# Strips for the left-over rows, four gate-and-up buffers and a new order of loads in a mixture-of-experts kernel

## The reference

```python
def _swiglu(x, w_gu, w_down):
    f = w_down.shape[0]
    gu = x @ w_gu
    return (jax.nn.silu(gu[..., :f]) * gu[..., f:]) @ w_down
...
    def body(b, acc):
        rows = lax.dynamic_slice(row_tok, (b * EXPERT_BLOCK,), (EXPERT_BLOCK,))
        rw = lax.dynamic_slice(row_w, (b * EXPERT_BLOCK,), (EXPERT_BLOCK,))
        e = block_e[b]
        gu = x_pad[rows] @ w_gu[e]
        y = ((jax.nn.silu(gu[:, :f]) * gu[:, f:]) @ w_down[e]) * rw[:, None]
        return acc.at[rows].add(y)
...
    routed = _routed_experts(xt, idx, w.astype(xt.dtype), w_gu, w_down)
    shared = _swiglu(xt, sh_w_gu, sh_w_down)
    return (routed + shared).reshape(B, L, D)
```

## Time and profile before

| | us |
|---|---|
| three runs | 1251.51, 1248.92, 1253.96 |
| median | 1251.51 |
| the profiled execution | 1256.82 |
| its span in the trace | 1255.0 |
| PE busy in the span | 1189.5 (95%) |
| DVE busy in the span | 787.9 (63%) |
| first product of the experts' loop starts | 439.87 |
| down(0) starts | 458.25 |
| up of the last step starts | 1182.38 |

### The profile page before, as it was taken

How to read it: one execution, slowest core, us unless ns; L and a number is a source line. 1 busy time by engine, 2 the same in 40 slices (tenths; PEclk the granted TensorE clock), 3 DMA queues, 4 the chain that set the end, 5 groups by cost and what they waited for, 6 DMA issues and landing times.

```text
span 1255.0 us, 22626 instructions
## 1 busy us (share of the span) xinstructions
PE 1189.5 (95%) x7122; PEld 1040.6 (83%) x7122; DVE 787.9 (63%) x1625; ACT 420.8 (34%) x582; POOL 606.0 (48%) x509
## 2 busy tenths in 40 slices
PE   6999999999999799999999999999999999999973
PEld 6897989747874399999999999999999998998931
DVE  7565657388988256666665566566566655647528
ACT  5253435353441023233333233233232232323323
POOL 5222222001657455666555666666666665756310
PEclk9999999999999999999999999999999999999997
DMA  6111111403352979999999999999999999999864
GB/s 240 51 35 51 44 41 34 184 27 135 102 169 71 278 230 352 375 364 359 370 355 366 357 351 362 358 349 367 344 352 355 343 352 338 346 350 341 282 165 175
DMA packets 83587, 317.50 MB, mean 253 GB/s; under 512 B 15989, under 2 KB 32450, under 8 KB 58594
## 3 DMA queue, kind: packets, MB, share of 16 engines
q1 hardware_dynamic: 56592, 249.50, 51.4%
q0 software_dynamic: 26656, 67.23, 21.9%
q10 hardware_dynamic: 306, 0.34, 0.1%
HBM read 274.38 MB, written 51.00 MB: 259 GB/s over the span
## 4 chain that ended last, share of the span: by engine, by line
DMA 50%; PE 24%; issue 11%; DVE 9%; ACT 3%; POOL 3%; POOLq 1%; DVEq 0%; ACTq 0%; SPq 0%
DMA routed_rows<-ysb,to_row 47%; PE bank L116 6%; PE bank L117 6%; PE bank L118 6%; PE bank L957 3%; PE bank L440 2%; POOL expert_list L787 1%; DMA win_raw<-in_w_in 1%; POOL routed_rows L840 1%; DVE routed L1440 1%; DVE h L1136 1%; DVE routed L1429 1%; DMA lists<-expert_list 1%; DVE h L1134 1%; DVE h L1120 1%
## 5 line engine op out<-in xcount | busy, mean ns | idle before, releaser
L957 PEld LDWEIGHTS bank<-xT,wgu 128*128 128x128 f32 x4096 | 516.3, 192 | 21.2 <-issue 10.4
L957 PE MATMUL bank<-xT,wgu 128*128 128x160 f32 (+1 forms) x4096 | 521.0, 288 | 10.5 <-DVE xT L1317 9.6
L810 POOL DMA_INDIRECT xg<-h_rows,from_row x288 | 324.2, 1126 | 110.6 <-issue 86.7
L840 POOL DMA_INDIRECT routed_rows<-ysb,to_row x96 | 147.8, 1540 | 215.8 <-issue 210.3
L1098 ACT ACTIVATE ysb<-bank,of_row 128x512 f32<-128x512 f32 x64 | 44.0, 687 | 439.3 <-DVE to_row L1312 381.1
L1359 DVE TENSOR_TENSOR wd_lo<-wd_raw,wd_hi 128x1024 fp32r<-128x1024 f32 x128 | 151.1, 1222 | 39.9 <-ACT wd_hi L1089 39.4
L1089 ACT ACTIVATE wd_hi<-wd_raw 128x1024 fp32r<-128x1024 f32 x128 | 127.9, 1048 | 1.4 <-issue 0.6
L787 POOL DMA_INDIRECT expert_list<-entry,place x64 | 64.7, 1010 | 129.9 <-DVE place L1197 112.2
L116 PE MATMUL bank<-hT_hi,win_hi 128*128 128x348 f32 (+1 forms) x320 | 113.4, 355 | 9.7 <-DVE hT_lo L538 9.7
L352 POOL TENSOR_TENSOR win_lo<-win_raw,win_hi 128x1024 fp32r<-128x1024 f32 x16 | 43.6, 2725 | 145.6 <-ACT win_hi L463 145.5
L1302 DVE TENSOR_TENSOR picks<-lists,pick 128x20 f32<-128x20 f32 x64 | 11.9, 185 | 161.5 <-POOLq L834 111.0
(11 more groups left out here) (216 smaller groups left out, 1629.5 us busy)
## 6 DMA issues: line engine op xcount, KB each, us to landing
wgu<-in_w_gu SPq DMA_DIRECT2D x128, 1024.0 KB
wd_raw<-in_w_down SPq DMA_DIRECT2D x64, 1024.0 KB, 8.4
win_raw<-in_w_in SPq DMA_DIRECT2D x16, 512.0 KB, 3.9
xg<-h_rows,from_row POOLq DMA_INDIRECT x288
hT_raw<-in_hT SPq DMA_DIRECT2D x8, 520.0 KB, 7.4
wout_raw<-in_w_out SPq DMA_DIRECT2D x1, 4096.0 KB, 14.4
h_in<-in_h_rows SPq DMA_DIRECT2D x8, 512.0 KB, 4.0
h_rows<-h SPq DMA_DIRECT2D x8, 512.0 KB, 2.7
```

Of the source, the lines that this page charges most:

```text
L810: pool.indirect_dma_start(out=xg[b][:, g, :], out_offset=None, in_=h1_quarters, in_offset=bass.IndirectOffsetOnAxis(ap=from_row[b][:, g:g ...
L840: pool.indirect_dma_start(out=routed_rows, out_offset=bass.IndirectOffsetOnAxis(ap=to_row[b][0:r, half:half + 1], axis=0), in_=ysb[b][0:r, ...
L957: mm = pe.matmul(bank[:, 2 * f + half, 0:BLOCK[b]], wgu[b][:, f, k, c:c + P], xT[b][:, k, 0:BLOCK[b]], start=(k == 0), stop=(k == KT - 1))
```

## The change

1. **Left-over rows.** The 32 rows get a tile of their own, hid_rest (plain float32, not split), and are multiplied by wd_raw, which wd_lo of even steps no longer overwrites. There are four matmuls for c and k = 0, 1, each with a stationary operand of 32 columns, and each writes 32 partitions of its own: k and c choose the strip at partition 0, 32, 64 or 96 (`rest_at`). They stand behind all of the step's main products. ACT and DVE add the two strips of each c as before. hid_hi becomes 128 columns wide, and POOL's clearing of it is gone.
2. **Four gate and up buffers.** SP loads the gate and up weights of step t + 4 after down(t), behind the down weights of step t + 2. The loop body holds four steps, and the number of steps is rounded to a multiple of four (64 stays 64).
3. **The loop's entry.** Of the loads at `first_ready` the first four stay; the second half of wgu1 and wd_raw1 wait for `lists_loaded`, the rest of the lists for the first step's gathers (`gathered0`), and wgu2 and wgu3 follow (wgu3 after the shared products). sdn and ln_f are loaded before `first_ready`. On DVE the second shared product's gating stands behind turn(0), and PE waits for it only at the second half of up(0).
4. **The lists' shape.** COLS goes from 65 to 72 and SLOTS from 36 to 33.

The diff, cut to its core:

```diff
-SLOTS = 36
+SLOTS = 33
 MORE_MAX = -(-(SEQ - P) // P)
-COLS = E + 1
+COLS = E + 8
...
+WGU = 4
...
-    wgu = [m.at(f"wgu{j}", 16384 * j, [P, FT, KT, 2 * P], F32) for j in range(2)]
+    wgu = [m.at(f"wgu{j}", (0, 16384, 166432, 99584)[j], [P, FT, KT, 2 * P], F32)
+           for j in range(WGU)]
     wd_at, wd_hi_at = (32768, 182816), (40960, 141184)
     wd_raw = [m.at(f"wd_raw{j}", wd_at[j], [P, FT, D], F32) for j in range(2)]
-    wd_lo = [m.at(f"wd_lo{j}", wd_at[j], [P, FT, D], F32R) for j in range(2)]
+    wd_lo = [m.at(f"wd_lo{j}", (132992, wd_at[1])[j], [P, FT, D], F32R) for j in range(2)]
...
-    hid_hi = [m.at(f"hid_hi{j}", (129152, 96416)[j], [P, FT, 2 * P], F32R) for j in range(2)]
+    xT = [m.at(f"xT{j}", (85888, 91680)[j], [P, KT, SQ * GB[j]], F32) for j in range(2)]
+    hid_hi = [m.at(f"hid_hi{j}", (129152, 96416)[j], [P, FT, P], F32R) for j in range(2)]
+    hid_rest = m.at("hid_rest", 130176, [P, FT, REST[0]], F32)
...
+    def rest_at(c, k):
+
+        return (2 * c + k) * SQ
...
+    def wgu_loads(i, j):
+
+        return i * 16 // WGU + j // WGU * 16 + 16
...
-        with eng.Fori(0, n, 2) as i:
-            for b in range(2):
-                yield i, b, 4
+        with eng.Fori(0, n, WGU) as i:
+            for j in range(WGU):
+                yield i, j, 4
...
+        sp.wait_ge(h1_stored, 16 * TILES)
+        sp.wait_ge(routed_begun, 16 * TILES)
+        sp.wait_ge(turned, TILES)
+        sp.dma_start(sdn[:, :, :], sh_down.rearrange("(k p) c -> p k c", p=P)
+                     ).then_inc(sdn_loaded, 16)
+        for j in range(2):
+            sp.dma_start(ln_f[j][:, :], ln[2 + j:3 + j, :].to_broadcast([P, D])
+                         ).then_inc(lnf_loaded, 16)
...
         load_wgu(0, 1, 0)
+        sp.wait_ge(lists_loaded, 16 * NQ)
         load_wgu(0, 1, 1)
-        sp.wait_ge(h1_stored, 16 * TILES)
-        sp.wait_ge(routed_begun, 16 * TILES)
         load_wd(0, 1)
-        sp.wait_ge(lists_loaded, 16 * NQ)
+        sp.wait_ge(gathered[0], 16 * GB[0])
         for q in range(NQ):
             sp.dma_start(lists[q * SQ:(q + 1) * SQ, FIRST:, :],
                          expert_list.rearrange("(a c) w -> a c w", a=SQ)[:, FIRST:, :]
                          ).then_inc(lists_rest_loaded, 16)
-        for f in range(FT):
-            sp.wait_ge(up_done, UPS + 2 * f + 2)
-            load_wgu(0, 2, f)
+        load_wgu(0, 2, 0)
+        load_wgu(0, 2, 1)
+        sp.wait_ge(sh_up, 2 * FT)
+        load_wgu(0, 3, 0)
+        load_wgu(0, 3, 1)
         sp.wait_ge(sched_loaded, 16)
         for i, j, more in steps(sp):
-            for f in range(FT if more >= 3 else 0):
-                sp.wait_ge(up_done, (i + j) * UPS + 2 * UPS + 2 * f + 2)
-                sp.sem_inc(sp_pass, 1)
-                load_wgu(i, j + 3, f)
             if more >= 2:
                 sp.wait_ge(down_done, DOWNS[1] + before(DOWNS, i, j + 1))
                 sp.sem_inc(sp_pass, 1)
                 load_wd(i, j + 2)
-            if more == 2:
-                sp.wait_ge(sh_up, 2 * FT)
-                sp.dma_start(sdn[:, :, :], sh_down.rearrange("(k p) c -> p k c", p=P)
-                             ).then_inc(sdn_loaded, 16)
-                sp.dma_start(ln_f[:, :, :], ln[2:4, :].unsqueeze(0).to_broadcast([P, 2, D])
-                             ).then_inc(lnf_loaded, 16)
+            for f in range(FT if more >= 4 else 0):
+                load_wgu(i, j + WGU, f)
...
-            pool.memset(hid_hi[b][:, :, :].bitcast(F32), 0.0).then_inc(hid_clear, 1)
-            pool.memset(hid_lo[b][:, :, :].bitcast(F32), 0.0).then_inc(hid_clear, 1)
...
-        pe.wait_ge(sh_ready, FT)
...
+                pe.wait_ge(wgu_loaded[j % WGU][f], wgu_loads(i, j))
                 pe.sem_inc(pe_pass, 1)
+                if of_first and f == 1:
+                    pe.wait_ge(sh_ready, FT)
...
-                for c in range(2 if REST[b] else 0):
-                    if first:
-                        pe.wait_ge(y_dve, YS[1] + before(YS, i, j))
-                    pe.matmul(bank[:, 6 + c, :], hid_hi[b][:, k, P:2 * P], w[c][0],
-                              start=first, stop=False)
-                    mm = pe.matmul(bank[:, 6 + c, :], hid_hi[b][:, k, P:2 * P], w[c][1],
-                                   start=False, stop=last)
-                    if last:
-                        mm.then_inc(down_done, 1)
-
-
-        up(0, 0)
+            if REST[b]:
+                pe.wait_ge(y_dve, YS[1] + before(YS, i, j))
+            for c in range(2 if REST[b] else 0):
+                for k in range(FT):
+                    at = rest_at(c, k)
+                    mm = pe.matmul(bank[at:at + REST[b], 6 + c, :], hid_rest[:, k, :],
+                                   wd_raw[b][:, k, c * 512:(c + 1) * 512],
+                                   start=True, stop=True)
+                mm.then_inc(down_done, 1)
...
-                act.activation(y_rest[0:REST[b], c, :], bank[LO:LO + REST[b], 6 + c, :],
-                               ACT.Copy, scale=of_row[b][LO:LO + REST[b], 1, 1:2]
+                at, to = rest_at(c, 1), rest_at(c, 0)
+                act.activation(y_rest[to:to + REST[b], :], bank[at:at + REST[b], 6 + c, :],
+                               ACT.Copy, scale=of_row[b][at:at + REST[b], 1, 1:2]
...
+        s.step(dve.tensor_scalar(sched_i[:, 4:5], sched_i[:, 4:5], 2, 2, ALU.logical_shift_right,
+                                 ALU.logical_shift_left))
...
+            if REST[b]:
+                dve.tensor_tensor(hid_rest[:, f, :], gact[:, f, P:n], up[:, P:n], ALU.mult)
...
-        gate_shared(1)
         turn(0, 0)
         rows_from(0, 2)
+        gate_shared(1)
```

## The result

The changed kernel takes 1265.99 us (median of 4 runs, 1264.44 to 1268.84) against 1252.64 us for the kernel before beside it: a ratio of 1.0114, interval 1.0084 to 1.0144. It is 1.1% slower. The forecast was 1243.4 us and a range of 1234 to 1263: wrong in direction, and the time lies 3 us outside the range. The profiled execution took 1264.44 us, its span is 1262.7 us.

The account below looks back on a forecast made before the run. PE, the stores and the DMA engines were taken to bound the loop within 3%. Entry -11, loop +4.9 and tail -2 sum to -8.1 us, from 1251.5 to 1243.4 us; range 1234 to 1263.

Parts of the forecast that it names:

- What bounds the kernel: In the experts' loop, PE, the stores and the DMA engines lie within 3%; cutting one alone gives little.
- the requests at 0: In the loop, four buffers and three weight requests issued together cost 0, bounds 0 to +16 us.
- The strips: Left-over rows' 32-column products bring PE to 23.76 us a pair of steps; the loop costs 4.9 us.
- 2.15 + 0.2: PE time added per pair: 2.15 us for four partly overlapping strip products, 0.2 us for changing shape.
- rival 2: In the loop, all four strips overlap, PE needs 22.5 us, stores bind early; about 1240 us, chance 0.13.
- order rule: Strip matmuls' starts stay in order; a strip's second record runs beside the next one's first: 2.15 us a pair.
- The entry: Before the loop, earlier lists and gathers and less lost clock give 11 us, bounds 6 and 12.
- the 0.7 us of stall before up(1): At the entry, PE waits 0.7 us for xT(1), ready between 436 and 442, wanted at 439.6.
- rival 4: The entry moves without shrinking: lists' rest fully delays step 1's gathers, clock falls; gain 6, 1248 us, chance 0.06.
- The tail: After PE's last down product, the last stores are less far behind: 2 us gained, bounds 0 and 4.3.
- rival 3: In the loop, the request burst or gathers keep stores at 24.3 us a pair; about 1261 us, chance 0.07.

Follow-up runs that it names:

- g_pause: a_paced plus sixteen empty GpSimd instructions, about 1 us, between a store's landing and the next store's issue; 1286.02 us, ratio 1.0219.
- h_norest: The changed kernel with spaced weight requests, without the store of the left-over rows; 1220.23 us, ratio 0.9735.
- n_less: a_paced without loading the second gate and up half of every odd block in the loop, 1 of 6.3 MB a pair; 1214.99 us, ratio 0.9694.
- a_paced: The changed kernel with the loop's weight requests spaced as in the kernel before; four buffers, strips and entry stay; 1248.29 us, ratio 0.9979.
- b_strips: The kernel before with only the new left-over rows' code (four 32-column products) added; 1255.57 us, ratio 1.0013.
- k_finer: a_paced with each gate and up half asked for in two requests of 64 partitions; 1561.62 us, ratio 1.2447.
- l_halfdown: a_paced without loading 64 of 128 partitions of the down weights in even blocks from the third block on; 1290.04 us, ratio 1.0325.
- i_best: The changed kernel with a_paced's requests, the lists' rest fetched beside their first part, weights of blocks 2 and 3 after block 1's gathers; 1254.15 us, ratio 1.001.
- c_nostrips: The changed kernel with the left-over rows multiplied as in the kernel before, in 128-column form; 1269.37 us, ratio 1.0109.
- f_gu_first: The changed kernel, requests still bunched, but gate and up halves asked for ahead of the down weights; 1251.89 us, ratio 1.0003.

## Why the prediction was wrong, point by point

**What bounds the kernel.** Right, and it mattered more than I let it: PE, stores and DMA engines within 3%. g_pause, h_norest and n_less confirm chain and engine load together as the limit behind PE.

**The step that failed: the requests at 0.** The text said that three requests together change "when 3 MB are queued, not how much", and that "the stores' landing of about 10 us should stay". The landing rose by 0.39 us in the mean (9.72 to 10.11), since when is what matters to a store: its first packet comes 4.1 us after the issue instead of 2.3. I had bounds for it, 0 to +16 us from the two paces of the stores, and put the value at the end without a row that said so. It was worth 17 us (a_paced against after). The upper bound was too low as well: 24.56 us a pair lies above 24.32, the worst pace that the trace of before shows. A trace of a kernel with spaced requests cannot bound what a bunch does.

**The strips.** The mechanism was right, the size off, and it did not matter. Each strip product has two records, and all eight of an even step ran within 1.06 us in the changed kernel:

```profile
933.29 0.40 PE L120 MATMUL bank<-wd_hi,hid_lo 128*128 128x512 f32 x1
933.62 1.06 PE L997 MATMUL bank<-wd_raw,hid_rest 128*32 128x512 f32 x8
934.61 0.40 PE L970 MATMUL bank<-xT,wgu 128*128 128x160 f32 x1
```

From the record ahead to the next up pass 1.32 us, 0.99 of them behind the first strip record. A pair takes 22.56 = 23.28 - 1.87 + 1.15 us where I had 2.15 + 0.2 for the last term. So all four products run at once (rival 2's bound, 0.86, plus 0.3 for the change of shape, inside the 0 to 0.6 given). Two shorter windows of the same timeline show how, in two waves of four records:

```profile
933.62 0.64 PE L997 MATMUL bank<-wd_raw,hid_rest 128*32 128x512 f32 x4
...
934.07 0.61 PE L997 MATMUL bank<-wd_raw,hid_rest 128*32 128x512 f32 x4
```

Within a wave the starts are 7 ns apart, and the second wave starts 0.45 us behind the first. Only records of the second wave, the second and the fourth, signal down_done, as the second product of each c does in the code. So I read the first wave as the first records of all four products, the second wave as their second records. The reason against rival 2, that both records of a product use the same columns, held (the second starts 0.45 us behind the first, near the 0.44 us of the earlier trace rows) and was no obstacle. What failed is the assumption that the first record of a strip waits for the second record of the strip ahead. The rule of the Trainium skill, "TensorE: Matmul & The Clock Gate", Part 3, that products on different column groups run concurrently, agrees with this row; my use of its order rule, that a strip's first record starts only beside the second record of the one ahead, does not. b_strips shows that the whole gain ends behind the stores. The forecast could not see that, because it had PE at 23.76, by chance the stores' own pace.

**The entry: 11 us forecast, 3 us found.** From the issue of the lists' first part the lists took 417.02 - 410.83 = 6.2 us (before 11.0; forecast 5 us less: right), up(0) came after 18.2 us (before 26.5; forecast 8.9 us less, 8.2 found: right). The failed term is the 0.7 us of stall before up(1). It was 5.82 us, and 9.57 - 7.3 = 2.3 us of clock on top, both beyond the bound of 3 and 2 in sum. The text had the right cause and the right window, xT(1) "ready between 436 and 442": it came at 442.9. DVE makes hidden(0) behind that, so PE could start only at 443.80. The 0.7 was taken from the middle of a window of 6 us, though every row on that transfer said that it holds up the gathers beside it. That was rival 4 (gain 6, chance 0.06), and it too was too kind. The two up products are also 0.5 us longer than the 8.6 and 7.1 us I had: 8.93 and, at full clock, 7.3.

**The tail.** 1.2 us gained, 2 forecast, within 0 to 4.3. The last store goes out 3.7 us behind the end of PE's last down product (1216.53 and 1212.85), where it was 7.8 us (1208.62 and 1200.80): less far behind, as forecast. But that is so since PE is held up by the stores, and from up(62) to that end it takes 33.0 us instead of 29.9. The reason given, a PE at 23.76 that the stores can follow, was wrong.

**The rivals.** What happened is rival 2's PE (22.5 us a pair) with rival 3's stores (24.3 us). Rival 3 had the mechanism, "the burst of requests", the mark (over 24.1 us past step 22) and nearly the time, 1261 us against 1266, at a chance of 0.07. Its terms were +21 for the loop and -11 for the entry where +15 and -6 were found, so that the nearness of its time is in part luck. I held against it that at 23.76 between pairs the stores had kept up; that was evidence on spaced requests only.

## What to carry to other kernels

When a chain of small dependent transfers and large loads share the DMA engines, the moment at which a load is asked for is a cost of its own: look at what was asked for in the few microseconds before each link, and price a change of it from both groups, not at nothing. A gain on an engine that others follow within 3% is a gain only up to the next pace, so the pace of the second and third must be known under the new timing. At a loop's entry follow the first link of the binding chain, here the first store in GpSimd's queue, and not the first product.

## What the hardware showed that I had not expected

- Requests of 64 partitions are slow. The same 8 KB packets took 0.51 us in the mean instead of 0.33 (k_finer against a_paced), a request of 512 KB landed after 23.2 us in the median, with what it waited in the queue, and the whole moved 248 instead of 350 GB/s; in l_halfdown 512 KB took 9.9 us beside 8.7 for 1024 KB.
- Transfers with larger packets starve those with smaller ones beside them: during the lists' rest (16 KB packets, 0.85 us each at first and 1.17 us in the mean) no gather packet of 4 KB started from 429 to 433 us in the changed kernel, and the first part of the lists (2.9 KB packets) took 17 instead of 6.2 us beside it in i_best.
- Four plain float32 products of 32 columns, two records each, ran within 1.06 us, as two waves of four records, where eight records one after another at the pitch of rows 5 would take 3.5.
- A loop timed by such a chain can scatter, and a few runs do not tell how much: the changed kernel's four runs lie within 4 us, the four of c_nostrips, which has the same slow loop, within 16 us, the ten of f_gu_first within 15 us, and 23 of the kernel before within 12 us.
